# Last block of a fused Trainium2 kernel: gate and up tiles from x times norm weight, with two shift columns and the inverse rms applied to the products

## The reference, cut to what matters

```python
def _rms_norm(x, g):
    xf = x.astype(jnp.float32)
    y = xf * lax.rsqrt(jnp.mean(xf * xf, axis=-1, keepdims=True) + EPS)
    return (y * g.astype(jnp.float32)).astype(x.dtype)

def _modulate(h, shift, scale):
    return h * (1 + scale) + shift

def _conv_ffn(h, rows, w_up, conv_w, conv_b, w_down):
    a, val = _split(h @ w_up, (D_FF_2, D_FF_2))
    img = a.reshape(bsz, rows, length // rows, D_FF_2)
    a = lax.conv_general_dilated(img, conv_w[:, :, None, :], (1, 1), 'SAME', ...) + conv_b
    return (jax.nn.gelu(a.reshape(bsz, length, D_FF_2), approximate=False) * val) @ w_down

hx2 = _modulate(_rms_norm(x, norm2_g[l]), sh2x, sc2x)
x = x + g2x * _conv_ffn(hx2, rows, ffn_w_up[l], ffn_conv_w[l], ffn_conv_b[l], ffn_w_down[l])
```

## Time and profile before

| | us |
|---|---|
| median of 3 runs (lowest, highest) | 1193.85 (1192.24, 1193.92) |
| the profiled execution | 1193.65 |
| its span in the profile | 1192.3 |
| PE busy | 1153.8 (97%) |
| PE weight load busy | 1105.0 (93%) |
| DVE busy | 833.1 (70%) |
| ACT busy | 617.4 (52%) |
| POOL busy | 149.2 (13%) |
| last block's feed-forward part, first gate tile to last down tile | 980.2 to 1178.7 |

### The profile page before, as it was taken

One profiled execution on the slowest core, in us unless ns is written; L12 is line 12 of the kernel. 1 busy time (PEld: TensorE's weight loads), 2 busy tenths in 40 slices (PEclk: granted clock), 3 DMA queues, 4 the chain that ended last, 5 costly groups with the idle time before them and its releaser, 6 DMA issues.

```text
span 1192.3 us, 21814 instructions
## 1 busy us (share of the span) xinstructions
PE 1153.8 (97%) x8998; PEld 1105.0 (93%) x8998; DVE 833.1 (70%) x1291; ACT 617.4 (52%) x933; POOL 149.2 (13%) x111
## 2 busy tenths in 40 slices
PE   7999899999989999999999999999999988999996
PEld 6989899999988899999999788989999988999995
DVE  5767588878675756877777666587546767777775
ACT  5655444445656655444444655756447455555553
POOL 0002100000100003000000000000000032444441
PEclk9999999999999999999999989999999989999998
DMA  8645478776534344888888535354335653555640
GB/s 310 228 144 180 150 242 292 241 255 197 175 110 138 124 163 139 286 281 278 280 266 274 192 108 175 107 178 158 107 102 164 194 161 121 181 177 177 194 142 36
DMA packets 60322, 221.36 MB, mean 186 GB/s; under 512 B 6736, under 2 KB 6992, under 8 KB 59840
## 3 DMA queue, kind: packets, MB, share of 16 engines
q1 hardware_dynamic: 59760, 218.53, 56.0%
q10 hardware_dynamic: 288, 1.05, 0.2%
q0 software_dynamic: 176, 0.39, 0.1%
HBM read 218.90 MB, written 1.05 MB: 184 GB/s over the span
## 4 chain that ended last, share of the span: by engine, by line
PE 87%; DVE 6%; ACT 4%; issue 1%; DMA 1%; SPq 0%; POOL 0%; ACTq 0%; DVEq 0%
PE PS L359 25%; PE PS L361 24%; PE PS L360 24%; PE PS L364 14%; ACT w_hi L850 2%; DVE w_lo L1330 2%; DVE PS L1928 1%; DVE SQ L1363 1%; DMA ARENA<-memT 1%; DVE H_lo L1373 0%; PE PS L613 0%; ACT ARENA L947 0%; DVE Y_lo L1369 0%; DVE ARENA L1956 0%; DVE ARENA L1363 0%
## 5 line engine op out<-in xcount | busy, mean ns | idle before, releaser
L1330 DVE TENSOR_TENSOR w_lo<-raw,w_hi 128x1024 fp32r<-128x1024 f32 x325 | 398.4, 1227 | 194.8 <-ACT w_hi L850 194.2
L850 ACT ACTIVATE w_hi<-raw 128x1024 fp32r<-128x1024 f32 x356 | 372.0, 1054 | 146.9 <-PE PS L361 122.8
L359 PE MATMUL PS<-Y_hi,w_hi 128*128 128x256 f32 x1240 | 358.3, 289 | 12.9 <-DVE Y_lo L1369 5.9
L360 PE MATMUL PS<-Y_lo,w_hi 128*128 128x256 f32 x1240 | 353.3, 285 | 0.0
L361 PE MATMUL PS<-Y_hi,w_lo 128*128 128x256 f32 x1240 | 353.1, 285 | 0.0
L359 PEld LDWEIGHTS PS<-Y_hi,w_hi 128*128 128x128 f32 x1240 | 239.9, 193 | 21.2 <-issue 8.6
L360 PEld LDWEIGHTS PS<-Y_lo,w_hi 128*128 128x128 f32 x1240 | 240.4, 194 | 0.4 <-issue 0.2
L361 PEld LDWEIGHTS PS<-Y_hi,w_lo 128*128 128x128 f32 x1240 | 240.2, 194 | 0.0
L359 PE MATMUL PS<-H_hi,w_hi 128*128 128x256 f32 x768 | 221.1, 288 | 5.9 <-DVE w_lo L1330 2.8
L361 PE MATMUL PS<-H_hi,w_lo 128*128 128x256 f32 x768 | 217.9, 284 | 0.0
L360 PE MATMUL PS<-H_lo,w_hi 128*128 128x256 f32 x768 | 217.9, 284 | 0.0
(11 more groups left out here) (233 smaller groups left out, 1364.4 us busy)
## 6 DMA issues: line engine op xcount, KB each, us to landing
raw<-stream SPq DMA_DIRECT2D x404, 512.0 KB, 4.2
ARENA<-memT SPq DMA_DIRECT2D x2, 512.0 KB, 7.8
X<-xT SPq DMA_DIRECT2D x1, 1024.0 KB, 11.4
ARENA<-ctxT SPq DMA_DIRECT2D x1, 1024.0 KB, 5.8
ARENA<-memT SPq DMA_DIRECT2D x1, 1024.0 KB, 8.1
outT<-ARENA SPq DMA_DIRECT2D x2, 512.0 KB, 2.6
CROW<-c_rows SPq DMA_DIRECT2D x1, 512.0 KB, 9.4
ARENA<-c_rows SPq DMA_DIRECT2D x1, 512.0 KB, 11.9
```

What stands on the lines that cost most here:

```text
L359: pe.matmul(o, wh, xh, start=start, stop=False, skip_group_check=True)
L360: pe.matmul(o, wh, xl, start=False, stop=False, skip_group_check=True)
L850: act.activation(w_hi[n % RING][:], raw[at][:], ACT.Copy).then_inc(*mark("hi", n))
L1330: dve.tensor_tensor(w_lo[n % RING][:], raw[raw_of("slot", n)][:], w_hi[n % RING][:], ALU.subtract).then_inc(*mark("lo_dve", n))
```

## The change

- The last block has no norm pass. During w_o2, after each residual tile, ACT writes the high part of X times GS (norm weight times 1 + scale) into U_hi and DVE the low part into U_lo, as blocks 0 and 1 do for theirs. The gate and up tiles multiply these. The sum over partitions for the rms is issued inside the first gate tile, before its seventh chunk.
- U has T + 2 = 258 columns per chunk. Columns 256 and 257 hold the modulation's shift, so column 256 of each product is shift times W. They are written once by ACT (`shift_hi`) and DVE (`shift_lo`) before w_o2.
- On DVE each gate and each up tile is multiplied in place with the inverse rms (`scaled`), and its shift column is copied to a small buffer (`bias`). The image copy on ACT becomes an Identity with that bias and waits for both; the middle tap is now computed from the image and waits for it. `hidden` adds the up tile's shift in one three-operand instruction.
- The clearing of the image buffers moves ahead of w_o2.
- `context_silu` in block 0's first round moves behind the two fills.
- `beside` becomes `ahead` in stages b_q and ctx_v on DVE.

```diff
--- before.py
+++ after.py
@@ -105,6 +105,7 @@
     "stick_act": ("z_abs", "z_exp", "softplus", "a"),
     "decay_act": ("decay_abs", "decay_exp", "decay_ln", "kd_exp", "q_exp", "k_exp", "dec"),
     "conv_act": ("img", "conv_mid"),
+    "shift_dve": ("shift_lo", "scaled", "bias"),
     "gates_act": ("vs_gelu", "u_gelu", "sig_r", "sig_a", "sig_b"),
     "memory_dve": ("ma_max0", "ma_max", "ma_rc", "ma_prob", "ma_lo"),
     "stick_dve": ("z_kept", "minus_log_not", "log_not_first", "log_not", "log_a", "am_part", "am"),
@@ -232,7 +233,8 @@
         sb("below", [P, 15488])
         CX_lo, CX_hi = sb("CX_lo", [P, KC, T], F32R), sb("CX_hi", [P, KC, T], F32R)
         CX = (CX_hi, CX_lo)
-        sb("above", [P, 24832 - 19584])
+        U_lo, U_hi = sb("U_lo", [P, KC, T + 2], F32R), sb("U_hi", [P, KC, T + 2], F32R)
+        sb("above", [P, 24832 - 19584 - 2 * KC * (T + 2)])
 
         def area(at, *shape):
             n = int(np.prod(shape))
@@ -288,6 +290,9 @@
 
         H2, Y2 = Y, H
         RS_COLS = small[:, 32:34]
+        SHIFTED = small[:, 0:4]
+        SH2_COLS = MOD[:, 24:32, 0:1].to_broadcast([P, KC, 2])
+        U_TOKENS = (U_hi[:, :, 0:T], U_lo[:, :, 0:T])
         RS_OF = {"mem0": RS[:, 1], "mix0": RS[:, 0], "mix1": RS[:, 0], "ctx": LR[:, 1], "out": RS[:, 0]}
 
         def gain(name, c):
@@ -811,19 +816,19 @@
             side.finish()
             project("br_b", KC, H2, lambda i: ("br_b", i), None, [("ob_lo", c // 2) for c in range(KC)])
             project("w_o2", KC, Y2, lambda i: ("added", 2, i), None, [("merged_lo", i) for i in range(KC)])
-            residual_sum(2)
-
-            def conv_gate_up(j, ready=None):
+
+            def conv_gate_up(j, ready=None, within=None):
                 p = j % 2
                 claim(2 * p)
                 assert n == gate_slot(2, j)
-                tall(PS[:, 2 * p, 0:T], H2, ready)
+                tall(PS[:, 2 * p, 0:T + 2], (U_hi, U_lo), ready, within)
                 emptied[2 * p] = [("gelu", j)]
                 claim(2 * p + 1)
-                tall(PS[:, 2 * p + 1, 0:T], H2)
+                tall(PS[:, 2 * p + 1, 0:T + 2], (U_hi, U_lo))
                 emptied[2 * p + 1] = [("g_lo", 2, j)]
 
-            conv_gate_up(0, [norm_low("norm2", k) for k in range(KC)])
+            pe.wait_ge(*past("shift_lo"))
+            conv_gate_up(0, [("h_lo", 2, k) for k in range(KC)], lambda: residual_sum(2))
             conv_gate_up(1)
             for j in range(2, FC):
                 conv_gate_up(j)
@@ -984,12 +989,12 @@
                     act.activation(GF[:], GF[:], ACT.Silu).then_inc(*mark("silu", l, j))
                     if j == 0:
                         hidden(l, j)
-                    if j == 0 and l == 0:
-                        context_silu()
                     fill()
                     if beside:
                         beside.step()
                     fill()
+                    if j == 0 and l == 0:
+                        context_silu()
                     if beside:
                         beside.step()
                     if j:
@@ -1281,18 +1286,25 @@
                 act.activation(Y2[0][:, i], GB[:, i], ACT.Copy).then_inc(*mark("merged_hi", i))
 
             project("br_b", KC, left, then=merged_hi)
-            project("w_o2", KC, left, then=residual_square(2))
+            act.wait_ge(*past("gs", 2))
+            act.wait_ge(*past("mod", 3))
+            act.activation(U_hi[:, :, T:T + 2], SH2_COLS, ACT.Copy).then_inc(*mark("shift_hi"))
+            project("w_o2", KC, left, then=residual_square(2, U_TOKENS, lambda c: GS[:, 2, c:c + 1]))
             inverse_rms("res2")
-            whole(norm_his("norm2", H2, lambda c: SH2(c)))
             act.preload_act_table(ACT.Gelu)
 
             def conv_gate(j):
                 b = 2 * (j % 2)
                 img = PS[:, b, 0:T].rearrange("p (r c) -> p r c", r=ROWS)
+                inner = IMGS[:, j % 2, 1:ROWS + 1, 1:COLS + 1]
+                bias = SHIFTED[:, j % 2:j % 2 + 1]
                 act.wait_ge(*past("used", gate_slot(2, j)))
+                act.wait_ge(*past("scaled", j, 0))
+                act.wait_ge(*past("bias", j, 0))
                 act.wait_ge(*past("taps", j - 2, 7) if j > 1 else past("img_zero"))
-                act.activation(IMGS[:, j % 2, 1:ROWS + 1, 1:COLS + 1], img, ACT.Copy).then_inc(*mark("img", j))
-                act.activation(conv_sum(j), img, ACT.Identity, bias=gain("fconv_b", j),
+                act.activation(inner, img, ACT.Identity, bias=bias).then_inc(*mark("img", j))
+                act.wait_ge(*past("img", j))
+                act.activation(conv_sum(j), inner, ACT.Identity, bias=gain("fconv_b", j),
                                scale=gain("fconv", j + 4 * FC)).then_inc(*mark("conv_mid", j))
 
             def conv_value(j):
@@ -1871,7 +1883,7 @@
             kept = 0
             side.tasks = [both(memory_attention(1), chain(*side.tasks)),
                           both(stick_schedule(stick_group, lambda: kept), stick_outputs())]
-            beside(MC, side, 2)
+            ahead(MC, side, 2)
             dve.wait_ge(*past("mask_kept", 1))
             for i in range(MC):
                 kept += 1
@@ -1884,7 +1896,7 @@
 
             side = Side(block1_end())
             side.step()
-            beside(8, side, 2)
+            ahead(8, side, 2)
             side.finish()
             side = Side(both(context_states(), block1_output()))
             ahead(17, side)
@@ -1914,10 +1926,21 @@
                 dve.tensor_tensor(Y2[1][:, i], GB[:, i], Y2[0][:, i], ALU.subtract).then_inc(*mark("merged_lo", i))
 
             project("br_b", KC, branch_b, then=merged_low)
-            project("w_o2", KC, residual(2, lambda c: G1(c)))
+            dve.memset(IMGS, 0.0).then_inc(*mark("img_zero"))
             dve.wait_ge(*past("gs", 2))
-            whole(norms("norm2", X, lambda c: GS[:, 2, c:c + 1], ("res2", RS[:, 0]), H2, lambda c: SH2(c)))
-            dve.memset(IMGS, 0.0).then_inc(*mark("img_zero"))
+            dve.wait_ge(*past("mod", 3))
+            dve.wait_ge(*past("shift_hi"))
+            dve.tensor_tensor(U_lo[:, :, T:T + 2], SH2_COLS, U_hi[:, :, T:T + 2],
+                              ALU.subtract).then_inc(*mark("shift_lo"))
+            project("w_o2", KC, residual(2, lambda c: G1(c)),
+                    then=residual_low(2, U_TOKENS, lambda c: GS[:, 2, c:c + 1]))
+
+            def scaled(j, i):
+                half = PS[:, 2 * (j % 2) + i, 0:T]
+                dve.wait_ge(*past("used", gate_slot(2, j) + i))
+                dve.tensor_tensor(half, half, RS[:, 0], ALU.mult).then_inc(*mark("scaled", j, i))
+                at = 2 * i + j % 2
+                dve.tensor_copy(SHIFTED[:, at:at + 1], PS[:, 2 * (j % 2) + i, T:T + 1]).then_inc(*mark("bias", j, i))
 
             def conv_taps(j):
                 dve.wait_ge(*past("conv_mid", j))
@@ -1931,15 +1954,20 @@
 
             def conv_value(j):
                 dve.wait_ge(*past("gelu", j))
-                dve.wait_ge(*past("used", up_slot(2, j)))
-                dve.tensor_tensor(up_product(j), PS[:, 2 * (j % 2) + 1, 0:T], GF[:],
-                                  ALU.mult).then_inc(*mark("hidden", 2, j))
-
+                dve.wait_ge(*past("bias", j, 1))
+                dve.wait_ge(*past("scaled", j, 1))
+                dve.scalar_tensor_tensor(up_product(j), PS[:, 2 * (j % 2) + 1, 0:T],
+                                         SHIFTED[:, 2 + j % 2:3 + j % 2], GF[:], ALU.add,
+                                         ALU.mult).then_inc(*mark("hidden", 2, j))
+
+            dve.wait_ge(*past("rs", "res2"))
             for j in range(FC):
+                scaled(j, 0)
                 if j:
                     conv_value(j - 1)
                 fill()
                 conv_taps(j)
+                scaled(j, 1)
                 fill()
                 if j:
                     hidden_low(2, j - 1)
```

## The result

The changed kernel takes 1205.49 us (median of 4 runs, 1203.87 to 1206.75) against 1193.39 us for the kernel before in the same comparison: ratio 1.0102, 95% interval [1.0084, 1.0119]. Slower, by 12 us (1%), where the prediction had 1190.3 and a range up to 1198. The profiled execution took 1203.87, its span is 1202.3. In it PE is busy 1153.5 us (96%), DVE 862.0 (72%), ACT 621.4 (52%), POOL 151.3 (13%).

What follows compares the result with a forecast made beforehand. PE was the bound before; in the changed last block's rounds DVE and ACT's joint queue becomes it. From 1193.65 us, -1.3 - 2.2 - 6.8 + 7.0 (last block) = -3.3 gives 1190.3, range 1181 to 1198.

Steps and rivals of the forecast that it cites:

- part 5: Last block's rounds: added DVE work makes even rounds 10.03 us, odd 8.29, a pair 18.32 against 17.26.
- Part 1: Block 0's first round, context_silu behind two fills: -1.3 us, bounds 0 and -2.6.
- Part 2: Stage b_q, side work ahead of the fill: PE's two waits go, -2.2 us, bounds 0 and -2.5.
- Part 3: Stage ctx_v, side work ahead of the fill: -3.4 us of waits, -6.8 in all with full clock.
- Rival D: Stage ctx_v: the side-work move gives only its waits, -3.0 for -6.8, so 1194 us; chance 0.12.
- Part 4: Last block's start, norm pass gone: up tile 2 starts 3.8 us earlier, after a 2.9 us wait for gelu 0.
- Rival A: Last block's rounds stay PE-bound: -3.5 us in the block, -13.8 in all, 1180 us; chance 0.14.
- Rival B: Last block's up tiles: waits for G_lo lower PE's clock, 0.8 us each, nine give 1197.5 us; chance 0.13.
- Rival C: Last block's rounds: added DVE scaled and copy take full durations, +5.1 us, 1195.4; chance 0.11.
- Two more columns at 1 us in all: Last block's gate and up matmuls: 0.001 us more each over 1056, 1 us in all, hidden under DVE's queue.

Runs made afterwards that it cites:

- e3: The kernel after, with one wait added so POOL's low-weight subtraction starts only when DVE's of the slot before is done: 1193.60 us.
- e1: The kernel before with only context_silu moved behind the fills and `ahead` in b_q and ctx_v, last block unchanged: 1184.85 us.
- e6: e3 with gelu and hidden of tile j - 1 ahead of tile j's image and scaling, and both product halves made early: 1175.10 us.
- e7: e6 with the last block's gate and up tiles at 256 columns instead of 258, leaving out the shift: 1173.46 us.
- e5: e3 with gelu of tile j - 1 ahead of tile j's image on ACT, and its hidden ahead of tile j's scaling on DVE: 1192.61 us.
- e8: e3 with one more low-weight subtraction per pair of rounds moved from DVE to POOL: 1188.31 us.

## Why the prediction was wrong

**The step that failed** is part 5, the length of the odd round: "an odd one 8.29, a pair 18.32". It adds up DVE's queue with every w_lo at 1.14 start to start and never asks where POOL's w_lo lies beside it once the round is re-timed. In the old timing the two passed each other; with the odd round stretched, ACT hands POOL its third slot just before DVE reaches its own. Seven meetings of 1.55 are 10.9 us of the 15.2 by which 1205.5 misses 1190.3, and e3, which keeps the two apart, gives 11.9 back. Whether the change loses hung on it: without the meetings it is at 1193.6, level with the kernel before and still not faster.

The trace of the kernel before had the meeting already, in a stage that the change does not touch: a w_lo of the same shape takes 2.01 there, and it ends 1.08 after the second of two POOL instructions (POOL, then DVE).

```profile
891.99 2.52 POOL L2036 TENSOR_TENSOR ARENA<-ARENA 128x512 f32<-128x512 f32 x2 [100.64 <-ACT ARENA L863]
...
893.58 2.01 DVE L1330 TENSOR_TENSOR w_lo<-raw,w_hi 128x1024 fp32r<-128x1024 f32 x1 [1.65 <-ACT w_hi L850]
```

The earlier trace rows held the same warning, and I read it as a price only: H_lo of block 0 takes 479 ns at least and 956 in the median, one instruction with two lengths. In w_o2 of the kernel after the same form (two inputs in SBUF, L1467) takes 0.48 before POOL has begun its square sums, and 0.96 once each runs beside one (DVE, POOL, DVE):

```profile
946.79 0.48 DVE L1467 SCALAR_TENSOR_TENSOR U_lo<-X,GS,U_hi 128x256 fp32r<-128x256 f32 x1
...
948.56 1.41 POOL L2013 TENSOR_TENSOR SQ<-SQ 128x256 f32<-128x256 f32 x1 [57.11 <-ACT SQ L969]
...
949.29 0.96 DVE L1467 SCALAR_TENSOR_TENSOR U_lo<-X,GS,U_hi 128x256 fp32r<-128x256 f32 x1
```

Each of the two holds the other here. POOL's instruction comes under DVE's w_lo of 948.14 to 949.37 and takes 1.41, where the last of its kind, at 965.30 with no w_lo beside it, takes 0.74. DVE's U_lo then stands until POOL's end at 949.97 and ends 0.28 later.

The Trainium skill says this outright, in SBUF — State Buffer, section SBUF: two separate sides: VectorE and GpSimd arbitrate for one pair of ports, an operation of VectorE with two SBUF inputs against one of GpSimd that reads SBUF, whichever starts first holds it for the whole instruction and the other is fully blocked. The trace agrees, with 2.77, 1.98 and 3.17 us by how much of POOL's instruction was left, and 4.15 for taps that read PSUM. One thing the records can't tell is who comes first when they begin within 0.03 us: at 1062.53 POOL's begins first and POOL is held. Applied to the forecast the rule would have been the missing rival, with up to nine meetings, one in each odd round, of up to 2.4 us each (an estimate, from POOL's 2.41 in the rows of the kernel before) as its price.

Point by point, by the times of PE's events in the two traces:
- Part 1, -1.3: right. The wait at 136.09 fell from 2.24 to 0.36, gate tile 3 came 2.06 earlier, of which 0.81 stood ahead of the block already (121.68 against 120.87): -1.25.
- Part 2, -2.2: right. Both waits at 357 and 363 are gone; the matmul at 371.48 is at 367.03, -2.4 after part 1.
- Part 3, -6.8: right, within 0.6. The copy of the k tile moved from 694.63 to 683.99, -6.2 after the parts before it; the clock is 1.00 in 682 to 688. In e1, with the clock at 0.73 there, the part gave 1.5 less. Rival D is wrong.
- Part 4, up tile 2 gains 3.8: it gained 4.3; the waits are 2.73 for gelu 0 and 2.54 for G_lo 0, forecast 2.9 for the first.
- Part 5, even round 10.03: 10.08. Odd round without the meeting, 9.96 less 1.55: 8.41 for 8.29. The image takes 0.48, where the nearest row had 0.51; the 0.48 that was worked out from the Trainium skill, ScalarE: Activation LUTs, section What ACT_TABLE_LOAD costs, agrees. The middle tap (conv_mid) takes 0.57 for 0.53.
- The sum without the meetings, 1190.3, against e3's 1193.6: a remaining 3.3. A pair of 18.49 for 18.32 is 1.6 of it. In e3's last two down tiles PE is granted 0.80 after a wait of 2.50 and takes 7.46 us for 48 matmuls, against 5.98 in the kernel after: 1.5 (windows of e3, then of the kernel after).

```profile
1170.46:1179.00 8.54, 7.46 (x48) 7.26 (x48) 1.65 (x5) 1.72 (x3) 0.00 (x0) 0.80 0.00 0
```

```profile
1182.52:1190.00 7.48, 5.98 (x48) 5.78 (x48) 2.07 (x6) 2.15 (x3) 0.00 (x0) 1.00 0.00 0
```

- Rival A, rounds bound by PE: wrong for this change, though e6 shows that with another order of the calls, and POOL's wait, the rounds are bound by PE. Rival B, the lower clock: it occurs (0.52 at 1045 to 1048) but is not the cause: of the seven waits of 2.20 five leave the clock at 1.00 (the one at 1104.46 among them), and the pairs behind them take 20.03 to 20.06 all the same; and e3 takes the time away by touching POOL alone. The prediction tied the lower clock to waits above 2.2 us. In the kernel after two waits of 2.20 (at 1045.24 and 1164.57) bring it and five equal ones do not, so the length of the wait alone does not decide it in these traces. Rival C, full durations of scaled and copy: the trace has 0.33 from scaled to copy, and 0.07 from copy to what follows; wrong.
- Two more columns at 1 us in all: e7 is 1.6 below e6, but by the two traces only some 0.3 of it lies in the rounds, so the term was too high if anything. It would matter only in e6, where PE is the bound.

The gain for which the last block was changed, the closed gap before its first tile, is real (4.3 us) but small beside what the re-timed rounds lose: with e1's 1184.9 as the base, the last block's edit costs 20.6 us as written, 8.7 with POOL ordered, and gains 9.8 with the round's calls reordered as well.

## What to carry to other kernels

When a change makes a queue longer by a microsecond, lay the timelines of the engines that can hold each other beside each other in the new timing. An instruction whose duration is far from the minimum of its group is a sign that this can happen. Where two engines exclude each other, an extra wait on the one with slack can pay (12 us here), and the length of the one's instruction sets the other's loss. An operation that is ready late should not stand in the queue ahead of work that is ready, and its consumer not at the round's end: against e3, e5 moved one of the two and gained 1 us, which is within what its runs spread, e6 both and gained 18.5.

## What the runs showed that I had not expected

- A stall of PE costs more than the trace's idle time: 0.53 shown, 0.81 lost a pair (e8 against e6); in e5 0.32 + 0.21 shown and 1.08 lost (18.30 against 17.22). Some 0.28 each beyond the number shown; matmuls are 0.12 apart but a lone one is recorded at 0.28, and the first after a wait at 0.39. A short stall can show no idle time at all: in the kernel after a pair loses 2.82 against e6 with one wait of 2.20 shown, and a second stall shows only as a matmul of 0.39 at 1113.42, with the next 0.22 behind it.
- The time that DVE is blocked by POOL stands inside its instruction's record, not in the idle column, so no list of waits shows it; only the duration does.
